# Position biases gathered in reversed key order and read backwards, and the last block's head sums placed between its projections

## The reference

```python
dist_w = (nband - 1) * Q_BLOCK + qi[:, None] - kj[None, :]
bias_w = tbl[rel_bucket(dist_w)].transpose(2, 3, 0, 1)[:, :, None]
logit_w = jnp.einsum("bgrnqd,bgnkd->bgrnqk", qw, kw).astype(f32) + bias_w
```

```python
q = rms_norm_2(q.reshape(b, s, D_HEADS, HEAD_DIM), q_gain)
k = rms_norm_2(k.reshape(b, s, D_HEADS, HEAD_DIM), k_gain)
bias = jnp.transpose(rpb[:, row_idx][:, :, col_idx], (0, 2, 3, 1, 4))
s_loc = jnp.einsum('bmqhd,brmkhd->bhmqrk', qr, kblk).astype(jnp.float32) * scale + bias[None].astype(jnp.float32)
```

## Time and profile before

| | us |
|---|---|
| time, median of 3 runs (lowest to highest) | 2430.49 (2427.76 to 2430.84) |
| profiled execution, its own time | 2430.21 |
| profiled execution, span from first to last instruction | 2428.4 |
| PE busy | 2339.0 (96% of the span) |
| DVE busy | 1485.5 (61%) |
| ACT busy | 920.6 (38%) |
| POOL busy | 247.4 (10%) |
| mean granted clock of PE, as a share of full speed | 0.978 |

### The profile page before, as it was taken

The page is one execution under the profiler, slowest core; times in us unless marked ns, Lnnn a source line. Parts: engine busy times, 40 slices in busy tenths (PEclk is TensorE's granted clock), DMA queues, the critical chain, the costliest instruction groups (busy, mean ns, idle before and its releaser), DMA issues.

```text
span 2428.4 us, 33804 instructions
## 1 busy us (share of the span) xinstructions
PE 2339.0 (96%) x14432; PEld 2028.5 (84%) x14432; DVE 1485.5 (61%) x1944; ACT 920.6 (38%) x1351; POOL 247.4 (10%) x235
## 2 busy tenths in 40 slices
PE   8999998889999999999989999999999999998999
PEld 7999885689998888889858888888888888877999
DVE  6584446577868777756765877434754433775544
ACT  6653335544454222124353322223422222544442
POOL 0030000111110101010010101100100100101110
PEclk9899997899999999999999999999999999999999
DMA  5444370164654445532202454222544322511553
GB/s 225 174 183 147 113 260 36 46 250 169 235 195 148 181 169 204 205 113 97 95 33 83 161 208 176 103 95 96 208 166 182 139 96 96 156 70 70 184 199 105
DMA packets 34834, 356.30 MB, mean 147 GB/s; under 512 B 3981, under 2 KB 6188, under 8 KB 8444
## 3 DMA queue, kind: packets, MB, share of 16 engines
q1 hardware_dynamic: 31788, 343.67, 38.1%
q0 software_dynamic: 2896, 10.46, 1.6%
HBM read 351.15 MB, written 1.13 MB: 145 GB/s over the span
## 4 chain that ended last, share of the span: by engine, by line
PE 87%; DVE 7%; ACT 3%; issue 1%; DMA 1%; SPq 0%; POOL 0%; POOLq 0%; DVEq 0%; ACTq 0%
PE psum L833 25%; PE psum L834 25%; PE psum L835 25%; PE psum L1123 2%; PE psum L881 1%; PE psum L882 1%; PE psum L883 1%; DVE ring_r L1808 1%; DVE rr L1818 1%; ACT arena_r L1352 1%; PE psum L1118 1%; PE psum L1031 1%; PE psum L1022 1%; PE psum L1148 1%; PE psum L1092 0%
## 5 line engine op out<-in xcount | busy, mean ns | idle before, releaser
L833 PE MATMUL psum<-arena_r 128*128 128x256 f32 (+1 forms) x3384 | 1131.1, 334 | 20.3 <-DVE zT_r L1848 8.3
L835 PE MATMUL psum<-arena_r,ring_r 128*128 128x256 f32 (+1 forms) x3384 | 1121.9, 332 | 0.0
L834 PE MATMUL psum<-zT_r,arena_r 128*128 128x256 f32 (+1 forms) x2656 | 863.3, 325 | 0.0
L1352 ACT ACTIVATE arena_r<-ring 128x2048 fp32r<-128x2048 f32 (+1 forms) x252 | 473.3, 1879 | 718.1 <-PE psum L835 684.0
L833 PEld LDWEIGHTS psum<-arena_r 128*128 128x128 f32 x3384 | 639.3, 189 | 94.7 <-issue 21.8
L835 PEld LDWEIGHTS psum<-arena_r,ring_r 128*128 128x128 f32 x3384 | 641.1, 189 | 68.3
L1808 DVE TENSOR_TENSOR ring_r<-ring,arena_r 128x2048 fp32r<-128x2048 f32 (+1 forms) x252 | 568.2, 2256 | 199.4 <-ACT arena_r L1352 198.6
L834 PEld LDWEIGHTS psum<-zT_r,arena_r 128*128 128x128 f32 x2656 | 505.7, 190 | 45.1
L834 PE MATMUL psum<-arena_r 128*128 128x256 f32 (+1 forms) x1304 | 423.5, 325 | 0.0
L1959 DVE CUSTOM_DVE_ANT_0 psum<-arena,cb 128x1024 f32<-128x1024 f32 x256 | 318.0, 1301 | 0.0
L834 PEld LDWEIGHTS psum<-arena_r 128*128 128x128 f32 x1304 | 245.9, 189 | 20.4
(11 more groups left out here) (287 smaller groups left out, 2020.4 us busy)
## 6 DMA issues: line engine op xcount, KB each, us to landing
ring<-in_wf SPq DMA_DIRECT2D x75, 2048.0 KB, 7.8
ring<-in_w SPq DMA_DIRECT2D x41, 2048.0 KB, 7.8
arena<-in_w SPq DMA_DIRECT2D x72, 1024.0 KB, 9.8
ring<-in_wf SPq DMA_DIRECT2D x10, 1536.0 KB, 6.8
ring<-in_w SPq DMA_DIRECT2D x5, 1024.0 KB, 5.4
arena<-strip_scratch POOLq DMA_DIRECT2D x1, 2048.0 KB, 9.7
arena<-rpb_scratch POOLq DMA_DIRECT2D x16, 128.0 KB, 11.5
xT<-in_x SPq DMA_DIRECT2D x1, 1024.0 KB, 5.7
```

The lines of the kernel that those rows point to most:

```text
L833: mm(b[c][:, at], whc, xh[:, k, at], start=(k == ks[0]), stop=False)
L834: mm(b[c][:, at], whc, xl[:, k, at], start=False, stop=False)
L835: last = mm(b[c][:, at], wlc, xh[:, k, at], start=False, stop=(k == ks[-1]))
L1352: A(W_hi[h % NHI][:, 0:n], ring[:, half_slot(h)], ACT.Identity).then_inc(sig("w_hi"), 1)
```

## The change

The strip is stored in the opposite order (`oh_rev`), and the rows of the second bias table are reversed on the host (`d["rpb"]`), so that each gather gives every partition the right query with its keys in descending order. DVE reads these tables backwards, with a step of -1 on the innermost dimension: in the 16 bias adds of NSA, straight from `B_stage`, and in two large adds into `O_nb`, straight from `O_stage`. The two sets of eight exchange products are gone, and with them the eight copies into `B_T`. NSA's probabilities `B_P` move to where `B_T` was.

Around this the order changes. The first NSA scores wait for `cmp_turn` rather than for the read-out of `cmp_kv`, and only the second half of the first unit waits for that read-out. ACT makes the first Gelu before the two `w_hi` of `mergeB0`. In the last layer the eight head sums are spread over three places: four after `od_k0`, two after `od_k1`, and two between `od_v0` and `od_v1`. Squares, roots and norms are spread to match. ACT waits for the two adds (`rpb_added`) before it overwrites `O_stage` with `O_v`.

```diff
        ("w2k", 256), ("w2v", 128), ("wa2", 512), ("tbl", 16)]
-CST = [("ones", 128), ("eps", 1), ("one", 1), ("eps64", 1), ("ident", 128), ("blk64", 128), ("flip", 128), ("rope_r", 128),
+CST = [("ones", 128), ("eps", 1), ("one", 1), ("eps64", 1), ("ident", 128), ("blk64", 128), ("rope_r", 128),
        ("valid_c", 2 * CMP_N), ("gla_mask", 128), ("scan_mask", S),
...
     put("oh_fwd", onehot(np.arange(512) - 271))
-    put("oh_rev", onehot(255 - np.arange(384)))
+    put("oh_rev", onehot(np.arange(384) - 127))
     t = np.arange(S)
...
-    def split(first, second, chunk, who, width=HALF, who2=None):
+    def split(first, second, chunk, who, width=HALF, who2=None, between=("", "")):
...
         for i, stage in enumerate((first, second)):
-            add(stage, None if i else chunk, who2 if i and who2 else who, "split")
+            if i and between[0]:
+                add(between[0], None, between[1])
+            add(stage, None if i else chunk, who2 if i and who2 else who, len(between[1]))
             halves.append((first, i, width, stage, len(who)))
...
     add("cmp_turn", None, "AA")
-    add("flip", None, "V" * 8)
     add("cmp_kv", None, "VV")
...
     split("od_q0", "od_q1", w8(W8_OD), "AA")
-    split("od_k0", "od_k1", w8(W8_OD + 1), "AA")
-    add("od_flip", None, "V" * 8)
-    add("od_qn", None, "A" * 8)
-    split("od_v0", "od_v1", w8(W8_OD + 2), "AAAA")
+    split("od_k0", "od_k1", w8(W8_OD + 1), "AA", between=("od_qn0", "A" * 4))
+    add("od_qn4", None, "A" * 2)
+    split("od_v0", "od_v1", w8(W8_OD + 2), "AAAA", between=("od_qn6", "A" * 2))
     split("od_xp0", "od_xp1", w8(W8_OD + 3), "AA")
...
-        if _free == "split":
-            CHUNKS.append((_chunk, "tiles_filled", len(WHO) + len(_who)))
+        if isinstance(_free, int):
+            CHUNKS.append((_chunk, "tiles_filled", len(WHO) + _free + len(_who)))
         else:
...
         B_gate_ = sb("nsa_gate", 2 * 48)
-        ARENA = 26112
+        ARENA = 26232
         arena_at = nc.sbuf_base
...
         CMP_AT = 4 * BANK
+        def od_sum(j):
+            return TILE["od_qn0"] + j if j < 4 else TILE["od_qn4"] + j - 4 if j < 6 else TILE["od_qn6"] + j - 6
...
         B_stage = area(B_stage_at, 16, S)
-        B_P = area(6144, 2108), area(8252, 2108)
+        B_P = area(B_T_at, 2108), area(B_T_at + 2108, 2108)
         B_hid = area(B_hid_at, 2, 2, 60)
...
                     for kr in range(4):
-                        row = kr - (2 * t + 1 - r) + 7
+                        row = kr - (2 * t + r) + 7
                         src = bass.AP(tensor=rpb_dram.tensor, offset=row * 128,
...
                     free(1 + 2 * a)
+                    if u == 0 and a == 1:
+                        wait_evac(pe, TILE["cmp_kv"] + 1)
                     if a == 1:
...
                 last.then_inc(filled, 1)
-            pe.wait_ge(sig("stage_in"), 16)
-            for i in range(8):
-                b = open_tile(TILE["flip"] + i)
-                mm(b[:, :], C("flip"), area(B_stage_at + i * BANK, BANK), start=True, stop=True)\
-                    .then_inc(filled, 1)
             wait_evac(pe, TILE["cmp_turn"] + 1)
...
             def nsa_ready():
-                wait_evac(pe, TILE["cmp_kv"] + 1)
+                wait_evac(pe, TILE["cmp_turn"] + 1)
                 pe.wait_ge(sig("kswap_in"), 32)
...
             split_part(h, b, HALF_TOK[1], zh, z_lo, filled, before=split_ready(8, 1), both=True)
+            def head_sums(j0, j1):
+                for j in range(j0, j1):
+                    b = open_tile(od_sum(j))
+                    nt = S if j < 4 else TOK
+                    pe.wait_ge(sig("head_sq"), 5 + j + 1)
+                    mm(b[:, 0:nt], C("blk64"), O_rt[j], start=True, stop=True).then_inc(filled, 1)
+            head_sums(0, 4)
             split_features(HALF_AT["od_k1"], TOK, zh, z_lo)
-            pe.wait_ge(sig("rpb_stage"), 16 * 16)
-            for i in range(8):
-                b = open_tile(TILE["od_flip"] + i)
-                mm(b[:, :], C("flip"), area(O_stage_at + i * BANK, BANK), start=True, stop=True).then_inc(filled, 1)
-            for j in range(8):
-                b = open_tile(TILE["od_qn"] + j)
-                nt = S if j < 4 else TOK
-                pe.wait_ge(sig("head_sq"), 5 + j + 1)
-                mm(b[:, 0:nt], C("blk64"), O_rt[j], start=True, stop=True).then_inc(filled, 1)
-            for c in range(2):
-                split_tokens(HALF_AT[f"od_v{c}"], 4, zh, z_lo)
+            head_sums(4, 6)
+            split_tokens(HALF_AT["od_v0"], 4, zh, z_lo)
+            head_sums(6, 8)
+            split_tokens(HALF_AT["od_v1"], 4, zh, z_lo)
             for c in range(2):
...
                 wait_evac(pe, TILE["od_xp1"] + 1)
-                wait_evac(pe, TILE["od_flip"] + 7)
...
-            w_hi(HALF_AT["mergeB0_0"])
-            w_hi(HALF_AT["mergeB0_1"])
             for i in range(2):
+                if i == 1:
+                    w_hi(HALF_AT["mergeB0_0"])
+                    w_hi(HALF_AT["mergeB0_1"])
                 copy_tiles(f"cmp_hid{i}", 1, lambda j: B_hT[0:60, i, :], nt=256, rows=60, func=ACT.Gelu_apprx_tanh)
...
             copy_tiles("od_q1", 2, lambda j: O_q[:, 2 + j, :])
-            for c in range(2):
-                w_hi(HALF_AT[f"od_k{c}"] + 2)
-                copy_tiles(f"od_k{c}", 2, lambda j: O_k[:, 2 * c + j, :], nt=TOK)
+            def head_squares(j0, j1):
+                for j in range(j0, j1):
+                    src = O_q[:, j, :] if j < 4 else O_k[:, j - 4, :]
+                    A(O_rt[j], src, ACT.Square).then_inc(sig("head_sq"), 1)
+            def head_roots(j0, j1):
+                for j in range(j0, j1):
+                    nt = S if j < 4 else TOK
+                    b = empty(od_sum(j))
+                    A(O_rt[j], b[:, 0:nt], ACT.Sqrt, scale=1.0 if j < 4 else 1.0 / HD,
+                      bias=C("eps64") if j < 4 else C("eps")).then_inc(evac["A"], 1)
+            wait_evac(act, TILE["od_q1"] + 1)
+            head_squares(0, 4)
+            w_hi(HALF_AT["od_k0"] + 2)
+            copy_tiles("od_k0", 2, lambda j: O_k[:, j, :], nt=TOK)
+            head_roots(0, 4)
+            wait_evac(act, TILE["od_k0"] + 1)
+            head_squares(4, 6)
+            w_hi(HALF_AT["od_k1"] + 2)
+            copy_tiles("od_k1", 2, lambda j: O_k[:, 2 + j, :], nt=TOK)
+            head_roots(4, 6)
             wait_evac(act, TILE["od_k1"] + 1)
-            for j in range(8):
-                src = O_q[:, j, :] if j < 4 else O_k[:, j - 4, :]
-                A(O_rt[j], src, ACT.Square).then_inc(sig("head_sq"), 1)
-            for j in range(8):
-                nt = S if j < 4 else TOK
-                b = empty(TILE["od_qn"] + j)
-                A(O_rt[j], b[:, 0:nt], ACT.Sqrt, scale=1.0 if j < 4 else 1.0 / HD,
-                  bias=C("eps64") if j < 4 else C("eps")).then_inc(evac["A"], 1)
-            for c in range(2):
-                w_hi(HALF_AT[f"od_v{c}"] + 2)
-                copy_tiles(f"od_v{c}", 4, lambda t: O_v[:, t, 256 * c:256 * c + 256], nt=256)
+            head_squares(6, 8)
+            act.wait_ge(sig("rpb_added"), 2)
+            w_hi(HALF_AT["od_v0"] + 2)
+            copy_tiles("od_v0", 4, lambda t: O_v[:, t, 0:256], nt=256)
+            head_roots(6, 8)
+            w_hi(HALF_AT["od_v1"] + 2)
+            copy_tiles("od_v1", 4, lambda t: O_v[:, t, 256:512], nt=256)
             for c in range(2):
...
                         nk = P * (t + 1)
-                        j0 = P if t == 0 else 0
                         s_ = psum[:, 4 * a * S:4 * (a + 1) * S].rearrange("p (j s k) -> p j s k", j=2, s=2)
                         s_ = s_[:, :, :, 0:nk]
-                        bias = B_T[:, 4 * g:4 * g + 4, j0:j0 + nk].rearrange("p (j a) k -> p a j k", a=2)[:, a]\
+                        bias = B_stage[:, 4 * g:4 * g + 4, 0:nk][:, :, ::-1].rearrange("p (j a) k -> p a j k", a=2)[:, a]\
                             .unsqueeze(2).to_broadcast([P, 2, 2, nk])
...
             w_lo(HALF_AT["mergeB0_1"])
-            for i in range(8):
-                b = empty(TILE["flip"] + i)
-                v.tensor_copy(area(B_T_at + i * BANK, BANK), b[:, :]).then_inc(evac["V"], 1)
             b = empty(TILE["cmp_kv"])
...
                 .then_inc(evac["V"], 1)
+            dve.wait_ge(sig("stage_in"), 16)
             attention(*NSA_U, B_P, B_y)
...
-            def head_norm(stage, j, x, rtile, gain):
-                wait_evac(dve, TILE[stage] + j)
+            def head_norm(tile, x, rtile, gain):
+                wait_evac(dve, tile)
                 link(v.reciprocal(rtile, rtile))
...
             for j in range(5):
-                head_norm("ev_qn", j, E_qk[:, j, :], E_rt[:, j, :], V("qg_ev") if j < 4 else V("kg_ev"))
+                head_norm(TILE["ev_qn"] + j, E_qk[:, j, :], E_rt[:, j, :], V("qg_ev") if j < 4 else V("kg_ev"))
                 if j == 1:
...
             ffn(3, TOK, 1, 0, lambda: mods(1, 1, 24, 72))
```

(38 more changed lines are left out.)

## The result

| | before | changed |
|---|---|---|
| median of the runs timed side by side (lowest to highest), us | 2429.12 (2426.82 to 2430.84) | 2414.37 (2412.67 to 2417.81) |
| ratio, 95% interval | | 0.9945 (0.9932 to 0.9958) |
| profiled execution, its own time | 2430.21 | 2414.95 |
| its span | 2428.4 | 2413.2 |

The ratio is 13.4 us less, 10.2 to 16.5; the forecast was 13.1 less. So the change makes the kernel faster by more than the 0.2% that the prediction set as its bound, and the middle of the forecast was close. Its two halves were not equally right, as the traces show.

The account below looks back on a forecast made before the run. PE, holding 87% of the chain, was taken to bound the kernel. First place -7.4 and last layer -5.7 sum to -13.1 us: from 2430.21 to 2417.1, stated as 2417.3 for the runs' median, range 2413 to 2425.

Parts of the forecast that it names:

- R5: Rival: a later stage bound by transfers swallows the first place's 7.4 us, giving 2424.7 us; chance 0.02.
- First place, -7.4: NSA, up to its first bias add: flips removed and order changed, 7.4 us less, bounds -6.6 and -8.4.
- the uncovered read-out of `cmp_turn`: NSA: ACT's read-out, hidden under the flips until now, comes onto the chain before `cmp_kv`; +0.4 us, bounds 0 and 0.8.
- the two edits of order: NSA: Gelu ahead of `w_hi`, -0.3 us; first scores no longer waiting for the read-out of `cmp_kv`, -0.4 us.
- Backward read, no extra: NSA's bias adds on DVE: a step of -1 keeps today's 696 and 1227 ns, no extra time.
- The bound from rows 6: Upper bound for backward bias adds: they cost like the wide steps, 1.65 and 1.66 ns an element.
- Last layer, -5.7: Last layer: flips -6.87 us, product type changes +0.8, wait ahead of `od_k1` +0.4; sum -5.7, bounds -6.9 and -4.9.
- the +0.8: Last layer's head sums: three handovers from plain float32 to `fp32r` products instead of one; +0.8 us, bounds 0 and 1.0.
- new wait: Last layer: `od_k1` needs banks freed by ACT's first two roots, so PE waits 0.4 us, bounds 0 and 1.
- Squares, DVE's queue, the waits for the table and the adds: Last layer: moved ACT and DVE work stays covered; two adds take 4.6 us, DVE's queue ends near 2137.2.
- R2: Rival: without the flips PE's clock drops in NSA's attention, 2419.8 to 2421.3 us; sign, stretch over 82 us; chance 0.10.
- R3: Rival: last layer's three head-sum groups each meet ACT behind a 1.9 us `w_hi`, losing 5.7 us, giving 2423; chance 0.04.

Follow-up runs that it names:

- e1: The kernel before with only the edits of the first place (NSA), the last layer as before; ratio to before 0.9973.
- e3: The changed kernel with both bias tables read forwards (step +1), so biases land on wrong keys; ratio to before 0.9944.
- e4: The changed kernel with the eight head sums in one group after `od_k1`, squares, roots and norms ordered as before; ratio to before 0.9963.
- e7: The changed kernel with six extra unread products on PE ahead of the second half of each NSA unit's scores; ratio to before 0.9941.
- e8: The changed kernel with DVE adds of various steps and lengths appended behind DVE's last work; one run, 2424.64 us.
- e9: The changed kernel with `od_xp0` and `od_xp1` ahead of `od_v0` and `od_v1`, two head sums between the xp halves; ratio to before 0.9931.
- e10: The changed kernel itself, run again beside the version with xp first; ratio to before 0.9935, median 2414.96 us.
- e11: The version of e9 with xp ahead of v, run again beside the changed kernel; ratio to before 0.9924, median 2411.74 us.

## Why the prediction was right, point by point

*The number.* That 13.1 met 13.4 was in part luck: the two edited stretches give 14.9, and the repeat gave 15.8. The times of runs sort by their mean granted clock. Over the 39 runs of the kernel before that stood beside the experiments, the ten at 0.978 average 2430.4 us and the thirteen at 0.981 average 2425.5. At equal clock the two kernels are 15.0 us apart (0.979: 2429.6 from eleven runs, 2414.6 from three of the changed kernel) and 14.3 (0.980: 2427.8 from four, 2413.5 from three), which is what the stretches say.

*What bounds the kernel.* Right. Both gains came from PE's own sequence, and no later stretch took them back: from `mergeB` to `od_k0` 1633.26 us before, 1632.80 after, and 1629.9 to 1636.2 over all profiles. R5 falls.

*First place, -7.4.* Measured -7.48 (25.09 to 17.61), and within 0.01 the same in the eight further profiles that have its edits whole (`e1`, `e3`, `e4`, `e7`, `e8`, `e9`, `e10`, `e11`). The parts: the flips 7.06; the uncovered read-out of `cmp_turn` 0.36 where 0.4 was charged; the two edits of order 0.84 where 0.7 was credited. They add up to 7.5.

*Backward read, no extra.* Right, and shown directly: 1226 and 1227 ns forwards and backwards. The bound from rows 6 was the price of distant neighbours, not of a step other than +1; it begins between 2 and 4 elements. The Trainium skill (Vector Engine (DVE) Microarchitecture Reference, section 5.1) lists how the engine streams an operand with a negative step as not measured; here it costs nothing extra.

*Last layer, -5.7.* Measured -7.39. This half was mis-sized, on the slow side. The step that failed is "Where a plain float32 product hands over to an `fp32r` one ... so 0.40 more" and the +0.8 built on it. In rows 8 the sums seem to take 2122.08 - 2117.32 = 4.76 us; at the flips' pace they need 5.1 to 5.2. The 0.40 was the missing end of the sums, counted twice. In the changed kernel the two groups of 512 columns are short by the same 0.4. The "new wait" of 0.4 ahead of `od_k1` came out at 0.05, and with the 0.07 at its first product the whole first group costs 0.1 more than its own time: ACT began the four roots right behind its read-out (2092.02), and two of them were done when the fourth sum was. The two terms of +1.2 came to +0.1, which is 1.1 of the 1.7 us; the other 0.6 is the pace of the `v` and `xp` products, for which the sum had no term and whose cause stays open.

*Squares, DVE's queue, the waits for the table and the adds.* Right: 4.49 us for the two adds, the queue ends 38.1 us after the read-out of `od_k0`, and no stall of PE. What the prediction didn't say is what the spreading itself is worth. It costed the head sums only as a burden; `e4_sums_together` shows that it earns 3.5 us.

*R2, the clock.* The size was estimated well: NSA's attention took 86.9 us at the highest clock and 91.4 at the lowest, with up to 2 us of scatter at one clock. But no profile ties it to the flips. It is spread between executions, and the 4.9 us between the two groups of runs above show that a good part of the 4 to 10 us between runs of one kernel goes with the clock. R2's sign of a stretch over 82 us was no sign: 82 us was the window of rows 11, and the kernel before itself has 91.4 from its first bias add to `mergeB`. The Trainium skill's rule that activity releases the throttle (TensorE: Matmul & The Clock Gate, Part 1) would have the products pay part of their way; no profile here shows that they do.

*R3.* No group of sums in the changed kernel cost more than 0.1 us beyond its own time.

## What to carry to other kernels

If an exchange of order is only there because a gather shifts upwards, let it run upwards on the other index and give the reader a step of -1: on DVE, with a float32 operand in SBUF, that was free, and steps of 2 and 0 are too, while 4 and more took about 1.7 times as long an element beyond the fixed part. Here the gathers shift the table up by one from partition to partition; no run tried a gather that shifts it down, which would do without the reversed read as well. When you take work out of a dense sequence, ask what it used to hide (here eight squares and a read-out) and move the next consumer apart from its producer in the same edit. Before you charge a change of instruction type, add the record before it and the record after it: a late second start can be the end of the first.

## What was unexpected

PE's records place the first product of 256 columns behind plain float32 ones of 512 columns 0.40 us early; behind sums of 256 columns, a first product of 512 shows no such shift. One stretch of 90 us varied by 4.5 us between profiles in which DVE and ACT did the same work, for the most part with the granted clock, and whole runs of one kernel went with their mean clock too. And the same `v` products at full clock took 22.2 us in the ten profiles with the head sums in three groups and 22.6 in the three with one group.
